# Half of the second output product first for all tiles, and GpSimd instead of VectorE for the first half's normalisation, in a fused encoder layer on one core

## The reference, cut to what matters

```python
def _layer_norm(x, g, b):
    mu = mean(x); var = mean((x - mu) ** 2)
    return (x - mu) * rsqrt(var + LN_EPS) * g + b

mixed = _mixer(x, ...)                    # mix = [y_conv, y_lru] (256 x 1024);  mixed = mix @ w_out
x = _layer_norm(DEEPNORM_ALPHA * x + mixed, ln1_g, ln1_b)
ffn = _moe(x, ...)                        # logits = x @ w_router; top 4 of 32 experts for each token
x = _layer_norm(DEEPNORM_ALPHA * x + ffn, ln2_g, ln2_b)
```

## Time and profile before

| | |
|---|---|
| median of 3 runs | 1023.18 us (1023.04 to 1024.12) |
| the profiled execution's own time | 1022.98 us |
| its span in the trace | 1021.2 us |
| granted TensorE clock, mean | 0.932 of full speed |
| busy: PE, PEld, DVE, ACT, POOL | 833.8, 361.4, 246.2, 74.9, 8.1 us |
| read from HBM | 420.27 MB, 413 GB/s over the span |

### The profile page before, as it was taken

One profiled execution on the slowest core, in us unless ns is written; L12 is line 12 of the kernel. 1 busy time (PEld: TensorE's weight loads), 2 busy tenths in 40 slices (PEclk: granted clock), 3 DMA queues, 4 the chain that ended last, 5 costly groups with the idle time before them and its releaser, 6 DMA issues.

```text
span 1021.2 us, 20147 instructions
## 1 busy us (share of the span) xinstructions
PE 833.8 (82%) x8431; PEld 361.4 (35%) x8432; DVE 246.2 (24%) x691; ACT 74.9 (7%) x176; POOL 8.1 (1%) x27
## 2 busy tenths in 40 slices
PE   9999879998659999987699986756876887955895
PEld 8885434333213434332134422211322332311432
DVE  2473712222111222221112211111111121210233
ACT  1030100000000000000000000000000000000010
POOL 1000000000000000000000000000000000000000
PEclk9999989999889999997899997788988997998998
DMA  9987699999999999999999999999999999999996
GB/s 337 414 336 322 263 426 427 427 427 429 429 428 428 430 427 429 429 429 427 428 426 426 429 429 429 427 427 431 427 427 429 429 427 427 431 427 429 428 429 289
DMA packets 38638, 421.69 MB, mean 413 GB/s; under 512 B 5894, under 2 KB 6338, under 8 KB 14044
## 3 DMA queue, kind: packets, MB, share of 16 engines
q1 hardware_dynamic: 36180, 420.89, 97.8%
q10 hardware_dynamic: 2392, 0.44, 0.2%
q0 software_dynamic: 48, 0.09, 0.0%
HBM read 420.27 MB, written 1.18 MB: 413 GB/s over the span
## 4 chain that ended last, share of the span: by engine, by line
DMA 54%; PE 38%; DVE 5%; issue 2%; DVEq 0%; SPq 0%; POOLq 0%; ACT 0%; POOL 0%
DMA dn_buf<-in_w_down_dram 54%; PE ps L988 12%; PE ps L1021 12%; PE ps L825 5%; PE ps L868 3%; PE ps L982 2%; PE ps L842 1%; DVE act_t L721 1%; DVE lin L716 1%; DVE lin L719 1%; DVE glu L713 1%; DVE lin L714 1%; PE ps L817 0%; PE ps L901 0%; PE ps L856 0%
## 5 line engine op out<-in xcount | busy, mean ns | idle before, releaser
L988 PE MATMUL ps<-gu_buf,rows_t 128*32 128x512 f32 x2880 | 368.2, 657 | 103.0 <-DMA gu_buf<-in_w_gate_up_dram 103.0
L988 PEld LDWEIGHTS ps<-gu_buf,rows_t 128*32 128x32 f32 x2880 | 94.4, 116 | 364.6 <-issue 199.3
L1021 PE MATMUL ps<-dn_buf,act_t 128*32 128x256 f32 x2848 | 172.8, 389 | 44.2 <-DMA dn_buf<-in_w_down_dram 36.0
L713 DVE TENSOR_SCALAR glu<-ps 128x256 f32<-128x256 f32 x45 | 19.1, 424 | 604.6 <-PE ps L988 604.6
L1021 PEld LDWEIGHTS ps<-dn_buf,act_t 128*32 128x32 f32 x2848 | 88.6, 111 | 116.3 <-DMA dn_buf<-in_w_down_dram 49.6
L982 PE MATMUL ps<-turned,bias_sel 128*32 128x512 f32 x360 | 50.0, 628 | 23.2 <-issue 23.2
L441 ACT ACTIVATE sig<-glu 128x256 f32<-128x256 f32 x45 | 18.8, 417 | 535.2 <-DVE glu L713 535.2
L825 PE MATMUL ps<-turned,gu_buf 128*128 128x256 f32 x256 | 55.6, 379 | 0.0
L938 PE MATMUL ps<-xs,onehot 128*32 128x256 f32 x736 | 51.4, 399 | 1.5 <-DVE onehot L700 1.5
L962 PE MATMUL ps<-mix,back 32*128 32x256 f32 x720 | 52.2, 404 | 0.5 <-ACT mix L445 0.5
L825 PEld LDWEIGHTS ps<-turned,gu_buf 128*128 128x128 f32 x256 | 48.6, 190 | 6.6
(11 more groups left out here) (233 smaller groups left out, 304.4 us busy)
## 6 DMA issues: line engine op xcount, KB each, us to landing
gu_buf<-in_w_gate_up_dram SPq DMA_DIRECT2D x128, 2048.0 KB, 29.6
dn_buf<-in_w_down_dram SPq DMA_DIRECT2D x62, 2048.0 KB, 13.7
gu_buf<-in_w_in_dram SPq DMA_DIRECT2D x4, 2048.0 KB, 18.7
gu_buf<-in_w_out_dram SPq DMA_DIRECT2D x2, 2048.0 KB, 16.4
dn_buf<-in_w_down_dram SPq DMA_DIRECT2D x2, 1024.0 KB, 26.7
xs<-in_x_dram SPq DMA_DIRECT2D x2, 512.0 KB, 3.8
gu_buf<-in_w_in_dram SPq DMA_DIRECT2D x2, 512.0 KB, 6.4
gu_buf<-in_w_in_dram SPq DMA_DIRECT2D x1, 1024.0 KB, 9.1
```

What stands on the lines that cost most here:

```text
L713: V.tensor_scalar(glu[:], half(HB, 0), SWIGLU_LIMIT, None, ALU.min).then_inc(S["glu_ok"], 1)
L988: ins = T.matmul(ps[SLOTS * j:SLOTS * (j + 1), HB, :], rows_t[:, k, :], gu_buf[:, b, k, :].rearrange("p (two n) -> p two n", two=2)[:, :, ...
L1021: ins = T.matmul(ps[SLOTS * j:SLOTS * (j + 1), YB, 0:QF], act_t[:, DK * m + q, :], weights[q][:, QF * j:QF * (j + 1)], start=(m == 0 and q ...
```

## The change

TensorE does blocks `n = 4, 5` of the second output product first, for all four tiles (eight products), and raises `wout_half`. Row 4 of the buffer is then no longer read, and SyncE loads this half of expert 1's chunk 2 (1 MB, semaphore `gu_half`) at that point, and the other 1 MB after `out_ps` at 4 as before. The product `wsum` moves behind these eight. Then each tile gets its blocks 6 and 7.

For the first token half, `centre` and `scale` leave DVE. POOL does them in place in `xs`, in six operations of 128x512: two of (x - mean) x rstd, two of x gain, two of + bias, with the second half's power between the first two and the rest. `gather_first` and the fourth `load_extra` wait for `half_ok`, the third `load_extra` for `half_gained`. `centred` and `x1_ok` now count the second half alone. On DVE the router's correction comes ahead of the residuals.

```diff
@@ SyncE
             load_gu(1, 1, 1)
+            row_src = gu_src[1].rearrange("p (k n) -> p k n", k=KT)
+            sp.wait_ge(S["wout_half"], 1)
+            sp.dma_start(gu_buf[:, 1, GK * 2, :], row_src[:, GK * 2, :]).then_inc(S["gu_half"], 16)
             sp.wait_ge(S["out_ps"], 2 * TH)
-            load_gu(1, 1, 2)
+            sp.dma_start(gu_buf[:, 1, GK * 2 + 1, :], row_src[:, GK * 2 + 1, :]).then_inc(gu_in[1][2], 16)
...
-            sp.wait_ge(S["centred"], 2 * TH)
+            sp.wait_ge(S["centred"], 2)
+            sp.wait_ge(S["half_gained"], 2)
             load_extra(0)
...
-            sp.wait_ge(S["x1_ok"], 2 * TH)
+            sp.wait_ge(S["x1_ok"], 2)
+            sp.wait_ge(S["half_ok"], 2)
             load_extra(1)
@@ GpSimd
-            for h in range(TH):
+            def rstd_of(h):
                 pool.wait_ge(S["var_ok"], h + 1)
...
+            rstd_of(0)
+            pool.wait_ge(S["rstd_ok"], 1)
+            pool.wait_ge(S["ln1_in"], 32)
+            first_half = [xs[:, 0, 512 * c:512 * c + 512] for c in range(2)]
+            for c, v in enumerate(first_half):
+                pool.wait_ge(S["vt_ps"], c + 1)
+                nc.gpsimd.tensor_scalar(v, v, small[:, 360:361], small[:, 374:375], ALU.subtract, ALU.mult).then_inc(S["half_scaled"], 1)
+            rstd_of(1)
+            for c, v in enumerate(first_half):
+                pool.wait_ge(S["half_scaled"], c + 1)
+                nc.gpsimd.tensor_tensor(v, v, late[:, 0, 512 * c:512 * c + 512], ALU.mult).then_inc(S["half_gained"], 1)
+            for c, v in enumerate(first_half):
+                pool.wait_ge(S["half_gained"], c + 1)
+                nc.gpsimd.tensor_tensor(v, v, late[:, 1, 512 * c:512 * c + 512], ALU.add).then_inc(S["half_ok"], 1)
@@ VectorE
-            for c in range(2):
-                centre(0, c, xs[:, 0, 512 * c:512 * c + 512], mixed(0, c), late[:, 0, :], S["centred"])
             residual(1, 0)
-            scale_0(0)
-            scale_0(1)
             link(residual(1, 1))
@@ TensorE
+            for n in range(CT // 2):
+                for h in range(TH):
+                    for c in range(2):
+                        ins = mixer_out(CT + n, h, c, n)
+            ins.then_inc(S["wout_half"], 1)
...
             for h in range(TH):
                 for c in range(2):
-                    for n in range(CT):
+                    for n in range(CT // 2, CT):
                         ins = mixer_out(CT + n, h, c, n)
                     ins.then_inc(S["out_ps"], 1)
@@ TensorE, gather_first
-                pe.wait_ge(S["x1_ok"], 2)
+                pe.wait_ge(S["half_ok"], 2)
...
-                pe.wait_ge(S["centred"], 4)
+                pe.wait_ge(S["centred"], 2)
@@ TensorE, ahead of expert 1
+            pe.wait_ge(S["gu_half"], 16)
```

More of the change, by code:

```diff
@@ L187, in trunk @@
             "softplus_ok", "gates_ps", "gate_sb", "tanh_ok", "tanh_kept", "sqrt_ok", "gelu_in", "gelu_sig", "ch_used",
-            "mix_lru", "mix_conv", "lru_out_ps", "out_ps",
-            "wsum_in", "wsum_ps", "wr_ok", "v_ok", "var_ok", "centred", "rstd_ok", "x1_ok", "vt_ps", "vt_sb", "lpart_ps", "lpart_sb", "logits_ps", "top_ok", "exp_in", "exp_ok",
+            "mix_lru", "mix_conv", "lru_out_ps", "out_ps", "wout_half", "gu_half",
+            "wsum_in", "wsum_ps", "wr_ok", "v_ok", "var_ok", "centred", "half_scaled", "half_gained", "half_ok", "rstd_ok", "x1_ok", "vt_ps", "vt_sb", "lpart_ps", "lpart_sb", "logits_ps", "top_ok", "exp_in", "exp_ok",
             "gates_ok", "gates_t_ps", "gates_t_ok", "sel_ok", "rank_ps", "closed_ok", "closed_ps", "bounds_ok",
@@ L592, in residual @@
                 return norm_stats(h, c)
[L594 to L598, removed]
             def centre_in_place(c):
@@ L605, in scale_in_place @@
             def scale_in_place(c):
-                dve.wait_ge(S["centred"], 2 + c + 1)
+                dve.wait_ge(S["centred"], c + 1)
                 v = xs[:, 1, 512 * c:512 * c + 512]
@@ L626, in choose @@
                 return V.match_replace(taken[:, h, :], top[:, h, :], lgx[:, h, :], TAKEN)
[L628 to L631, removed]
             dve.wait_ge(S["wsum_ps"], 1)
@@ L636, in _ @@
             V.memset(lgx[:, :, E:], NO_LOGIT)
-            for c in range(2):
-                centre(0, c, xs[:, 0, 512 * c:512 * c + 512], mixed(0, c), late[:, 0, :], S["centred"])
+            dve.wait_ge(S["ln1_in"], 32)
+            residual(0, 0)
+            link(residual(0, 1))
+            norm_variance(0, stats, S["var_ok"])
             residual(1, 0)
-            scale_0(0)
-            scale_0(1)
             link(residual(1, 1))
@@ L884, in turn_residual @@
                 ins.then_inc(S["vt_ps"], 1)
+            for n in range(CT // 2):
[3 more added lines that the diff above has]
+            ins.then_inc(S["wout_half"], 1)
+            pe.wait_ge(S["wsum_in"], 1)
+            T.matmul(ps[:, TB, 0:2 * E], gated[:, 0, :], small[:, 384:384 + 2 * E], start=True, stop=True).then_inc(S["wsum_ps"], 1)
             for h in range(TH):
                 for c in range(2):
-                    for n in range(CT):
+                    for n in range(CT // 2, CT):
                         ins = mixer_out(CT + n, h, c, n)
@@ L892, in _ @@
                         turn_residual(0, 1)
-                    if h == 0 and c == 0:
-                        pe.wait_ge(S["wsum_in"], 1)
-                        T.matmul(ps[:, TB, 0:2 * E], gated[:, 0, :], small[:, 384:384 + 2 * E], start=True, stop=True).then_inc(S["wsum_ps"], 1)
             def start_sum():
@@ L1000, in expert_block @@
                 if first:
-                    pe.wait_ge(S["x1_ok"], 2 * TH)
+                    pe.wait_ge(S["x1_ok"], 2)
                 gather().then_inc(S["rows_ps"], 1)
```

## The result

The changed kernel takes 1028.27 us in the median of 8 runs (1026.95 to 1031.8), the kernel before 1023.14 us (1022.97 to 1024.12). The ratio is 1.0053, with a 95% interval of 1.0043 to 1.0064. So it is slower by about 5 us, where 2.5 were forecast and 1027.5 was the end of the range. The profiled execution took 1027.25 us with a span of 1025.5; against the execution profiled before that is +4.27.

The account below looks back on a forecast made before the run. It took the issue of expert 2's first chunk, released by TensorE, to set when the byte-bound stream starts. Refill 0, order 0, relief 0 and GpSimd +2.5 on 1022.98 gave 1025.5 us, range 1023.0 to 1027.5.

Parts of the forecast that it names:

- What bounds the kernel: DMA queue: bytes set the time from 121 us on; the last gap ends when TensorE frees expert 2's first chunk.
- The early refill: First DMA gap: 1 MB moved earlier shortens it by 2.45 us, given back in full in the second gap: 0.
- The order on TensorE: Second output product: transposes move behind fourteen products without waiting, and the product still ends at 109.6 us: cost 0.
- VectorE's relief: Two `centre` and two `scale` removed from VectorE, where it had time waiting for TensorE: worth 0.
- GpSimd's six operations: First-half layer norm on GpSimd: four operations of 1.15 us disturb VectorE and make the first gather 2.5 us late.
- the upper bound of 2.16: GpSimd operation of 512 columns: at most 2.16 us, four times a TENSOR_SCALAR of 128 columns; covered for the first two.
- the engines take turns: GpSimd's four operations and VectorE's two second-half `centre` alternate, each for a whole operation; the forecast case, chance 0.45.
- the rival side by side: GpSimd and VectorE don't disturb each other ahead of the gather: 1023.0 to 1024.0, say 1023.4 us; chance 0.30.
- my sign of being wrong: VectorE's first second-half `centre` still starting at 112.22 and taking 0.74 us, or the stream's full rate beginning before 121.
- the middle of 2.0 and 3.0 us: First gather's delay: 2.0 us if the `centre` loses turns, 3.0 if small L649 loses one too; 2.5 taken.
- The sum: Every step behind the gather, to expert 2's first-chunk issue and the end, moves by the delay: +2.5 us.

Follow-up runs that it names:

- e4: The kernel before, with expert 2's first chunk loaded as two halves of 1 MB, the first as soon as its row is free: 1023.99 us, ratio 1.0009.
- e7: The changed kernel without GpSimd's two multiplications by the gain and two additions of the bias: 1022.74 us, ratio 1.0002 to the kernel before.
- e8: The kernel before, with expert 1's chunk 2 (2 MB) issued 3 us later, behind the router's last product: 1023.32 us, ratio 1.0005.
- e1: The kernel before, with the changed kernel's TensorE order and early refill only, all layer norm left on VectorE: 1026.67 us, ratio 1.0034.
- e2: The kernel before, with GpSimd's six operations and the moved router correction, but the old TensorE order and load: 1027.23 us, ratio 1.0048.
- e6: The kernel before, with sixteen GpSimd MEMSETs of 128x256 behind the second power, for which no gather waits: 1023.03 us, ratio 1.0003.
- e11: The changed kernel measured again, beside the other experiments: 1028.47 us, ratio 1.0060 to the kernel before.
- e3: The changed kernel with 12 instead of 4 idle TensorE products ahead of the first gather: 1025.86 us, ratio 1.0031 to the kernel before.
- e5: The kernel before, with eight GpSimd additions of 128x256 behind the second power, for which no gather waits: 1023.88 us, ratio 1.0012.

## Why the prediction was wrong

**What bounds the kernel.** Right. From 200 to 985 us the rate is 426 to 429 GB/s in all thirteen profiles, and in all but two of the experiments the span follows the issue of expert 2's first chunk. It left out that this issue has a second wait, for the block counts, which ends within 0.1 us of the first (e4).

**The early refill, 0.** Right, and shown from both sides (e7, e8). The transfer came where it was forecast, and was given back in the later gap. Only its reason was a little too strict: a load may end somewhat behind 121 us too (e8).

**The order on TensorE, 0.** Right in the changed kernel: the output products end at 109.6, and e7 is at the time of before.

**VectorE's relief, 0.** The step's number was right by luck, since its reason was wrong. I read VectorE's idle time in the old order, where the first half's layer norm lies in a pause. The new order takes that pause away. Without the relief it costs 3.8 us (e1). The zeros of the order and of the relief hold only together.

**GpSimd's six operations, +2.5 us.** This is the step that failed in size. The durations were near: means of 1.26 and 1.39 us for the 1.15 taken, though 2.08 for a TENSOR_SCALAR where I had said about 1; the upper bound of 2.16 covered it, and e7 shows that by itself it cost nothing. It did hold up the second power, so that the multiplications began 0.46 us later than forecast, behind the first `centre` and not ahead of it; in e2, where they began first, this `centre` lost a turn. The choice that the engines take turns was right, and the rival side by side was wrong. That the first `centre` would start at 112.22 and take 0.74 us was my sign of being wrong, and it came; but it was too narrow, since the turns were lost by other steps. I let turns be lost by the two `centre` and at most one small step, priced at the middle of 2.0 and 3.0 us. In the changed kernel three small steps of 0.2 us each lost a turn, the first `centre` none, and the gather came 3.1 us late. I looked at long operations, and a short one pays the same price: the rest of GpSimd's current operation. The Trainium skill (SBUF — State Buffer, section "Who interferes with whom") adds to the two-input rule that a TENSOR_SCALAR in a mode that uses both ports contends too. L657 at 1.04 us and L658 at 1.31 beside a reading GpSimd agree, and so do e6's 0.51 and 0.71 us beside a writing one; I had weighed only its rule on two inputs.

**The sum.** One term was missing. "Every step behind the gather moves with it" took those steps at their old durations. TensorE stood still for 2.7 us ahead of the gather, where it had been 0.45, and came back at half clock: 1.7 us in the profiled execution, 2.8 in e11, taken out by eight idle products in e3. With both corrected, 3.1 + 1.7 = 4.8 us at the issue, and 4.3 in the span. The forecast delay of 2.5 us alone meant some 0.45 + 2.5 = 2.95 us without work, which should have raised this question. (A slip that changes nothing: of 1024.7 to 1026.2 two thirds, not three quarters, lie above 1025.2.)

## What to carry to other kernels

In front of a stream that is bound by bytes, find the issue that ends the last gap of the queue, and the waits that end together there. Here, a load of 1 MB issued 8 us earlier (e7) and one of 2 MB issued 3 us later (e8) ahead of it changed nothing. Work given to GpSimd is not free for VectorE's chain even if nobody waits for GpSimd: a short VectorE step with two SBUF inputs, or a TENSOR_SCALAR from SBUF to SBUF, can wait for a whole GpSimd operation (0.8 to 1.1 us each in the changed kernel), so count steps and not their length. And when a delay leaves TensorE without work, price what comes behind it at the lower clock, or give it idle products for the whole of the new wait. Idle products are not free either: once the clock had fallen, they delayed the gather themselves (e1).

## What the runs showed of the hardware that I had not expected

- A GpSimd TENSOR_SCALAR with two per-partition scalars on 128x512 f32 takes 2.08 us, longer than a two-input TENSOR_TENSOR of the same shape (1.26 us without company, up to 1.52).
- Which VectorE step waits depends on a few tenths of a microsecond: with GpSimd's multiplication starting behind the `centre` (112.57 against 112.22) this kept its 0.74 us, with it starting just ahead (112.28 against 112.41) it took 1.68. GpSimd waits too: the multiplication that began under the `centre` took 1.52 us, the next 1.26.
- GpSimd MEMSETs, which read nothing, left two-input VectorE steps alone (0.74 and 0.22 us) and stretched TENSOR_SCALARs (0.30 to 0.51 us).
- After 2.7 us without work TensorE's granted clock was 0.56 over the next 3.9 us; after 0.93 us (e3) and 1.27 us (e5) the gather ran at full clock. In e1 it was 0.50 from 115.5 to 120.4, though the pauses ahead of the fall were only 1.58 and 0.53 us.
